# A convolution's work split around a weight tile's low part, and its transposes moved into the middle of a chunk

## What is computed

```
proj = jnp.dot(u, w_in)                       # (256, 2048) x (2048, 19064)
...
xbc = jax.nn.silu(causal_depthwise_conv(sxbc, conv_w, conv_b))
xs, bs, cs = jnp.split(xbc, [2048, 2048 + 512], axis=-1)
...
y = ssd_scan(xs, dt, a, bs, cs)
```

## Time and profile before

| | |
|---|---|
| time, three runs | 3383.39 us median (3381.95 to 3383.8) |
| span of the profiled execution | 3380.1 us |
| profiled execution's own time | not recorded apart; the runs lie 1.9 to 3.7 us above its span |
| PE busy | 3279.9 us, 97% |
| DVE busy | 2253.8 us, 67% |
| ACT busy | 1690.3 us, 50% |
| convolution tiles, layer 0 | 214.65 to 374 us of the span |
| convolution tiles, layer 1 | 1418.30 to 1574 us |
| granted TensorE clock, mean | 0.992 |

### The profile page before, as it was taken

One profiled execution on the slowest core, in us unless ns is written; L12 is line 12 of the kernel. 1 busy time (PEld: TensorE's weight loads), 2 busy tenths in 40 slices (PEclk: granted clock), 3 DMA queues, 4 the chain that ended last, 5 costly groups with the idle time before them and its releaser, 6 DMA issues.

```text
span 3380.1 us, 43397 instructions
## 1 busy us (share of the span) xinstructions
PE 3279.9 (97%) x17994; PEld 2845.1 (84%) x17994; DVE 2253.8 (67%) x2699; ACT 1690.3 (50%) x2090; POOL 46.8 (1%) x90
## 2 busy tenths in 40 slices
PE   4899999999999999999999999999999999999998
PEld 3789889888888878898898888888798899988887
DVE  7878878866676556786666676655577776544454
ACT  4455764643433445556646544334447865434343
POOL 0000000000000000000000000000000000000000
PEclk8999999999999999999999999999999999999999
DMA  9854566567777654444544577765545443455554
GB/s 403 325 187 174 200 252 252 197 232 273 270 278 277 227 206 175 175 152 175 185 175 164 185 264 268 277 220 190 196 183 191 181 165 131 174 213 198 188 188 147
DMA packets 102916, 719.29 MB, mean 213 GB/s; under 512 B 12176, under 2 KB 12256, under 8 KB 18752
## 3 DMA queue, kind: packets, MB, share of 16 engines
q1 hardware_dynamic: 93888, 675.38, 54.0%
q0 software_dynamic: 8256, 37.64, 3.1%
q10 hardware_dynamic: 576, 3.50, 0.3%
HBM read 710.08 MB, written 6.40 MB: 212 GB/s over the span
## 4 chain that ended last, share of the span: by engine, by line
PE 88%; DVE 7%; DMA 2%; ACT 2%; issue 1%; DVEq 0%; ACTq 0%
PE G L1277 81%; DVE LL L1875 2%; DMA RAW<-w_ada_turned_packed_dram 2%; PE BD L1389 1%; DVE S L2079 1%; PE BA L1416 1%; DVE RAW L1868 1%; PE BD L1451 1%; DMA KV<-in_x_dram 1%; PE BC L1402 0%; PE BE L1332 0%; DVE RAW L1886 0%; PE BA L1470 0%; PE BC L1470 0%; PE BC L1434 0%
## 5 line engine op out<-in xcount | busy, mean ns | idle before, releaser
L1511 ACT ACTIVATE HH<-RAW 128x2048 fp32r<-128x2048 f32 x546 | 1044.8, 1914 | 1096.7 <-PE G L1277 1019.1
L1875 DVE TENSOR_TENSOR LL<-RAW,HH 128x2048 fp32r<-128x2048 f32 x546 | 1248.0, 2287 | 370.5 <-ACT HH L1511 370.0
L1277 PE MATMUL G<-HH,UH 128*128 128x512 f32 x2496 | 994.2, 398 | 35.1 <-DVE LL L1875 23.4
L1277 PE MATMUL G<-LL,UH 128*128 128x512 f32 x2496 | 977.0, 391 | 0.0
L1277 PE MATMUL G<-HH,UL 128*128 128x512 f32 x2496 | 976.7, 391 | 0.0
L1277 PE MATMUL G<-UH,HH 128*128 128x256 f32 x2080 | 602.0, 289 | 5.7 <-DVE LL L1875 5.6
L1277 PE MATMUL G<-UH,LL 128*128 128x256 f32 x2080 | 588.8, 283 | 0.0
L1277 PE MATMUL G<-UL,HH 128*128 128x256 f32 x2080 | 588.7, 283 | 0.0
L1277 PEld LDWEIGHTS G<-HH,UH 128*128 128x128 f32 x2496 | 471.7, 189 | 137.4 <-DVE LL L1875 26.1
L1277 PEld LDWEIGHTS G<-LL,UH 128*128 128x128 f32 x2496 | 471.4, 189 | 100.4
L1277 PEld LDWEIGHTS G<-HH,UL 128*128 128x128 f32 x2496 | 471.7, 189 | 97.9 <-issue 2.9
(11 more groups left out here) (387 smaller groups left out, 2329.0 us busy)
## 6 DMA issues: line engine op xcount, KB each, us to landing
RAW<-in_w_in_packed_dram SPq DMA_DIRECT2D x402, 1024.0 KB, 4.8
RAW<-w_ada_turned_packed_dram SPq DMA_DIRECT2D x96, 1024.0 KB, 5.0
RAW<-in_w_out_packed_dram SPq DMA_DIRECT2D x48, 1024.0 KB, 4.8
RAW<-in_w_o_ssd_packed_dram SPq DMA_DIRECT2D x32, 1024.0 KB, 4.9
RAW<-in_w_o_fox_packed_dram SPq DMA_DIRECT2D x16, 1024.0 KB, 5.2
RAW<-in_w_o_dsa_packed_dram SPq DMA_DIRECT2D x16, 1024.0 KB, 4.8
RAW<-in_w_proj_a_packed_dram SPq DMA_DIRECT2D x16, 1024.0 KB, 4.8
RAW<-in_w_proj_b_packed_dram SPq DMA_DIRECT2D x16, 1024.0 KB, 4.8
```

Of the source, the lines that this page charges most:

```text
L1277: mm = pe.matmul(to, lt, rh, start=first, stop=end, skip_group_check=True)
L1511: a.activation(HH[g % NH][:, :n], RAW[buf(ch["f"])][:, :n], ACT.Copy).then_inc(*hi_done.up(g))
L1875: v.tensor_tensor(LL[buf(f)][:, :n], RAW[buf(f)][:, :n], HH[g % NH][:, :n].bitcast(F32), ALU.subtract).then_inc(*lo_done.up(g))
```

## The change

The gate product gets a token of its own, `conv_gate`. Between a tile's taps and this token the planner puts the pending `lo`. The ACT copy of tiles 16 to 23 moves with it in the list. The turn of tile `ct-1`, and its store by ACT, come after a `yield MID`, so they stand in the middle of the next chunk. The PSUM pair is marked free at the third tap of its last tile.

```diff
             for ct in range(jb * 4, jb * 4 + 4):
                 o.tok_block["conv", l, ct] = b
                 put("conv", l, ct)
+                o.lower()
+                put("conv_gate", l, ct)
+                if ct % 4 == 3:
+                    o.blocks[b]["free_by"] = ("conv_tap", l, ct, 2)
                 if 0 < ct <= 20:
+                    yield MID
                     put("conv_turn", l, ct - 1)
                     ended("conv_putd", l, ct - 1)
-                if ct % 4 == 3:
-                    o.blocks[b]["free_by"] = ("conv_silu", l, ct)
                 if ct == 23:
                     ended("conv_bc", l, ct)
                 yield
@@ ACT
             a.wait_ge(*conv_tap.at(l, ct, 2))
             a.activation(th, y, ACT.Tanh, scale=0.5).then_inc(*conv_tanh.up(l, ct))
+
+        def conv_gate(l, ct):
+            y = CV[ct % 2][:, 0:S]
             if ct >= 16:
                 a.wait_ge(*conv_silu.at(l, ct))
                 a.activation((BT if ct < 20 else CTT)[:, ct % 4, :], y, ACT.Copy, scale=0.5).then_inc(*conv_bc.up(l, ct))
@@ DVE
             taps(conv_tap, conv_main, (l, ct), ps, y, lambda j: PB[:, j * 24 + ct:j * 24 + ct + 1], [3, 2, 1, 0])
+
+        def conv_gate(l, ct):
+            y, th = CV[ct % 2][:, 0:S], CV[ct % 2][:, S:2 * S]
             v.wait_ge(*conv_tanh.at(l, ct))
             v.scalar_tensor_tensor(y, th, 1.0, y, ALU.add, ALU.mult).then_inc(*conv_silu.up(l, ct))
```

More of the change, by code:

```diff
@@ L1034, in hybrid_stack @@
     conv_tanh = count("conv_tanh", o.all("conv"))
-    conv_silu = count("conv_silu", o.all("conv"))
+    conv_silu = count("conv_silu", o.all("conv_gate"))
     conv_bc = count("conv_bc", [t for t in o.all("conv") if t[1] >= 16])
@@ L1835, in scalar_program @@
         todo = {"start": begin, "x_sum": x_squares, "hi": hi, "gate_cols": gate_cols, "x_in": x_in, "x_norm": x_norm, "norm": norm, "xn": xn, "u": u,
-                "m_split": m_split, "rope": rope, "hd": hd, "hd_turn": hd_store, "tok": tok, "silu": silu, "conv": conv,
+                "m_split": m_split, "rope": rope, "hd": hd, "hd_turn": hd_store, "tok": tok, "silu": silu, "conv": conv, "conv_gate": conv_gate,
                 "conv_turn": conv_put, "sz_gate": sz_gate, "sz_norm": sz_norm, "gate": gate, "split": split,
@@ L2439, in vector_program @@
                 "rope": rope, "x_norm": x_norm, "norm": norm, "am": am_v, "xn": xn, "u": u, "gate": gate,
-                "m_split": m_split, "hd": hd, "silu": silu, "conv": conv, "conv2": conv2, "sz_gate": sz_gate,
+                "m_split": m_split, "hd": hd, "silu": silu, "conv": conv, "conv_gate": conv_gate, "conv2": conv2, "sz_gate": sz_gate,
                 "sz_norm": sz_norm, "sz_put": sz_put, "merge": merge, "split": split, "split_scan": split_scan,
```

## The result

| | before | changed |
|---|---|---|
| time, five runs each | 3383.39 us median (3381.95 to 3384.34) | 3394.56 us median (3392.67 to 3396.32) |
| ratio, 95% interval | | 1.0035 [1.0023, 1.0046] |
| span of the profiled execution | 3380.1 us | 3390.9 us |
| its own time | | 3392.67 us |

The change makes the kernel 11.2 us slower. The forecast was about 3394 us, and 3391.0 us for the span. Three single runs, one of copy_moved_product_first (4699 us) and two of the kernel before (5693 and 13628 us), lay far outside the range of all others and are left out everywhere.

What follows compares the result with a forecast made beforehand. PE, busy 97% of the span, was taken as the bound, so only its waits count. Terms -2.3 - 2.3 + 5.6 + 9.9 = +10.9 us gave span 3391.0, time about 3394; range 3384 to 3400, forecast's own 3390 to 3398.

Steps and rivals of the forecast that it cites:

- The product's delay: On DVE in each tile, the gate product starts 1.65 us later behind the low part, bounds 1.56 and 1.71.
- The late cycles: Tiles 16 to 23: cycle grows from 5.17 to 6.82 us, or 5.36 to 7.0 where ACT stores a turned tile.
- Both late losses: Tiles 16 to 23 delay PE: loss 5.6 us in layer 0 and 9.9 us in layer 1.
- this wait comes some 7.5 us later in the span: Sign: PE's last wait for the head scaling, at 1587.99 before, comes some 7.5 us later.
- The rival of 3388.6 us: DVE and ACT catch up ahead of 1587.99; late losses only 6.5 and 3.3 us, +5.2 in sum; chance 0.15.
- The faster rival: ACT's copy is not the link, late cycle at or below 5.97 us; gains stand alone, -6.7 us, 3376.7; chance 0.08.
- The early gains: Early tiles: PE waits less for low parts, gain 2.3 us in layer 0 and 2.3 us in layer 1.
- turns in mid-chunk cost the same: A turn's two products cost PE the same in mid-chunk, within the 5.97 us chunk; cost 0.
- the early waits of layer 0 vanish: Sign: PE waits for the low part hardly at all at 226 to 238 us, where waits were 1.70 and 1.31.
- Turns and PSUM, taken as zero: Mid-chunk turns cost 0, in late cycles 0 to 0.2 us per tile; PSUM freed at last tap: cost and gain 0.
- The clock: Rival: one or two more half-clock stretches of PE add 1.7 to 3.4 us, 3396 to 3397.7; chance 0.10.
- The four terms: Early gains of 2.3 us per layer, late losses of 5.6 (layer 0) and 9.9 us (layer 1): sum +10.9.

Runs made afterwards that it cites:

- copy_moved_product_first: Kernel before with ACT's copy of tiles 16 to 23 behind the next high part and PSUM freed at the third tap; product still first; 3381.16 us, 0.9995.
- copy_behind_high: Changed kernel with ACT's copy of tiles 16 to 23 as its own token in mid-chunk, behind the next high part; 3373.81 us, 0.997.
- turn_in_middle_alone: Kernel before, old order, with only the turns of tile ct-1 and their stores moved to mid-chunk; 3383.09 us, 1.0.
- low_first_alone: Kernel before with only the low part put ahead of the gate product; turns in the slot, PSUM freed at the product; 3395.47 us, 1.0036.
- psum_at_last_tap_alone: Kernel before, old order, with only the PSUM pair marked free at the third tap of the block's last tile; 3383.03 us, 0.9997.

## Why the prediction was right

**The product's delay.** Taken as 1.65 us, bounds 1.56 and 1.71. ACT's wait at the copy grew from 0.49 to 2.12, so by 1.63 us. The step under it was an estimate, that a low part behind the last tap starts 0.40 us after it (bounds 0.34 and 0.49). In tile 22 of layer 1 the taps begin at 1571.49, 1572.01 and 1572.53, and the low part at 1572.93: 0.40 us behind a tap that itself takes 0.48. The product begins 2.20 us behind the low part, which itself takes 2.28. So both starts lie 0.08 us nearer than the durations; in the kernel before it was 0.09, with the low part 0.34 us behind a product of 0.43.

**The late cycles.** Taken as 7.0 and 6.82 us. Tiles 19 to 23 of layer 1 lie 6.97, 6.95, 6.81 and 6.79 us apart. In layer 0 tile 23 starts 371.93 - 321.48 = 50.45 us behind tile 16, before 45.63, which is the +4.8 at tile 23. Both late losses reached PE: 5.55 us for 5.6, and 9.56 for 9.9. In layer 1 the sum was too large by 0.2 at tile 20 (+3.1 for +3.3) and by 0.3 at tile 23 (+7.95 for +8.25), and kept that. The last wait for the head scaling grew only from 1.92 to 2.80 us; the rest of the delay had met PE earlier, in the waits for low parts. The prediction's sign that this wait comes some 7.5 us later in the span was wrong: it came 1598.99 - 1587.99 = 11.0 us later, as the prediction's own sum of 10.9 implies.

**The lag isn't absorbed.** The rival of 3388.6 us rested on DVE and ACT catching up behind the last tile. The scan starts 9.56 us late, so nothing was caught up. The faster rival named its own condition, that the link is ACT's copy; copy_behind_high removes that link and lands at 3373.8 us, where the rival had 3376.7. So the link is shown by a run, not only by the sum.

**The early gains.** Layer 1 gave 2.29 us for 2.3. Layer 0 gave 1.86 for 2.3, the one term mis-sized by more than a tenth. The chunk at 228.86 did start 1.46 us earlier (227.40; 1.5 was taken). The second step gave 0.6 instead of 0.8: 237.99 became 235.95, not 235.7. Before, the two products of a turn stood inside PE's idle time ahead of that chunk and cost nothing, and the term "turns in mid-chunk cost the same" was made on chunks without a wait. In mid-chunk they take PE's time: turn_in_middle_alone, with the old order, is 0.2 us longer in each early part. The kernel with the new order and the turns in the slot does not get this back (27.89 us against 27.55), since there the turns wait for the later product. That the turns are the missing part here is argued from these numbers and the timeline; no run shows it apart. Nor did the early waits of layer 0 vanish, as the prediction's signs had it: 1.04 and 0.62 us stayed, and only those of layer 1 went.

**Turns and PSUM, taken as zero.** Alone, both are zero to within about 0.1%. With the low part first, the two together are worth what low_first_alone lies above the changed kernel, 0.9 us, within the spread. ACT's store does wait for the turn in mid-chunk, 5.1 us in layer 1 as the list shows, but tiles 8 to 16 there take 57.64 us for 57.61, so PE lost nothing by it.

**The clock.** In the kernel before, the granted clock was 0.50 for 3.4 us right behind the last wait of 1.92 us. The rival was one or two more such stretches, estimated at half their length each, +1.7 to +3.4 us (3396 to 3397.7). They did not come: the clock records of the two profiles hold 58.8 us at half clock before and 59.0 after, with 2.0 us of each behind the end of its span. The new waits of 0.3 to 1.5 us ahead of the late chunks were followed by none. That such a stretch follows from a wait was not shown: other profiles below have the same wait with and without it.

**What was luck.** The four terms sum to 11.0 us for 10.9, but 0.4 us of gain that did not come stands against 0.3 us of loss that did not come either. And a half-clock stretch at layer 1's end, in one profile of the changed kernel and not in the other, moved that segment by 1.6 us (77.91 and 76.33), so a hit within 1 us is closer than the reasoning could promise.

## What to carry to other kernels

Filling an idle stretch with work from further down the list delays everything that was behind the stretch, here a 0.43 us product by 1.63 us. Before doing so, look at who waits for it on the other engine and what is queued behind that waiting instruction: a 1.90 us high part stood there, and so a late tile's cycle went from 5.17 us, less than PE's chunk, to 6.81 us, more than it. If the waiting instruction can be moved behind the work that it holds, do both: copy_behind_high takes 3373.8 us, 9.6 us less than before (8.2 when repeated, 3374.94 beside 3383.15), and 6 to 7 us of that are the new order's (3381.16 without it), the same order that cost 11 us with the copy where it was.

## What the hardware showed that was not expected

A wait of PE decides less about the clock than the earlier trace rows suggested. In psum_at_last_tap_alone the wait for the head scaling is 1.92 us, as before, and the stretch right behind it is at full clock:

```profile
1591.22 0.66 PE L1332 MATMUL BE<-CST,S 128*128 128x128 f32 x4 [1.92 <-DVE S L2036]
```

```profile
1591.50:1595.50 4.00, 4.00 (x26) 1.00 0.48 203
```

And in the same kernel a half-clock stretch appears in layer 0's early tiles, where the kernel before had none behind the same wait of 1.70 us at 228.86 (the granted clock of 228.80 to 232.20 was 1.00 there):

```profile
231.43 0.58 PE L1277 MATMUL G<-UH,HH 128*128 128x256 f32 x1 [1.70 <-DVE LL L1875]
```

```profile
231.40:234.80 3.40, 3.38 (x16) 0.51 0.46 195
```

This stretch cost nothing: tiles 0 to 4 take 29.39 us with it and 29.41 without. PE was slower there (the first product took 0.58 us, where it had taken 0.39), but it then waited less, 0.82 us instead of 1.31 for the next low part, and not at all for ACT, where it had waited 0.74. Behind layer 1's last tile a stretch of 3.4 us cost 1.6 us (77.91 and 76.33), about half its length.

In turn_in_middle_alone the wait at this place, ahead of 231.51, is one of 2.53 us, and half clock follows too:

```profile
231.40:234.80 3.40, 3.29 (x15) 0.51 0.50 210
```

In the clock records of these profiles such stretches are mostly 3.4 us or twice that long (in the kernel before 3.4 us from 77.3 on, 6.8 us from 725.8 on). Their total, counted as above, was 59.0 us in one profile of the changed kernel and 56.0 in the other, and their places differ. So a difference of a few microseconds between two profiles has to be read from the segment where it arises. What decides whether a stretch comes stayed open.
